# Front stage of a diffusion block: modulation loads in another order, shift 1 added behind the channel DFT

## The reference, cut to what matters

```python
mod = silu(c) @ w_mod + b_mod                      # c: one row of 2048, w_mod: 2048 x 12288 (96 MB)
sh1, sc1, g1, sh2, sc2, g2 = split(mod, 6)         # six vectors of 2048
h = rms_norm(x, norm_g[0]) * (1 + sc1) + sh1
y = real(fft over the 256 tokens and, within each of 8 groups, over 256 channels of h) @ fnet_w
x = x + g1 * rms_norm(y, norm_g[1])
h2 = rms_norm(x, norm_g[2]) * (1 + sc2) + sh2
x = x + g2 * rms_norm(relu(h2 @ w_mlp_in)**2 @ w_mlp_out, norm_g[3])
# second block: projections, two kinds of attention, output projection, MLP, final norm
```

## Time and profile before

| | |
|---|---|
| time, median of 3 runs | 2184.45 us (2181.9 to 2184.6) |
| profiled execution, first to last instruction | 2180.3 us |
| of it ahead of the MLP's steady run (to 308.4 us) | 308.4 us |
| of it after that | 1871.9 us |
| TensorE busy | 2038.3 us, 93% |
| VectorE busy | 1270.9 us, 58% |
| ScalarE busy | 1020.5 us, 47% |
| moved by DMA | 463.03 MB, 212 GB/s on the mean |

### The profile page before, as it was taken

How to read it: one execution, slowest core, us unless ns; L and a number is a source line. 1 busy time by engine, 2 the same in 40 slices (tenths; PEclk the granted TensorE clock), 3 DMA queues, 4 the chain that set the end, 5 groups by cost and what they waited for, 6 DMA issues and landing times.

```text
span 2180.3 us, 24124 instructions
## 1 busy us (share of the span) xinstructions
PE 2038.3 (93%) x9141; PEld 1667.9 (76%) x9141; DVE 1270.9 (58%) x1191; ACT 1020.5 (47%) x1346; POOL 23.0 (1%) x25
## 2 busy tenths in 40 slices
PE   3499469999999999998999999999999999999997
PEld 1378358888888888887778778788888888888886
DVE  7978986555655454456546556654544454454454
ACT  3043245444444544444556654554445444544543
POOL 0000010000000000000000000000000000000000
PEclk9699669999999999999999999999999999999999
DMA  9999977666675555555454454455555555555552
GB/s 400 420 348 358 333 251 252 236 234 242 232 248 174 191 186 194 183 193 174 136 174 159 152 172 143 166 174 193 183 194 187 188 192 192 178 189 194 190 186 103
DMA packets 193757, 463.03 MB, mean 212 GB/s; under 512 B 7401, under 2 KB 7849, under 8 KB 180753
## 3 DMA queue, kind: packets, MB, share of 16 engines
q1 hardware_dynamic: 191808, 455.11, 60.6%
q0 software_dynamic: 848, 3.70, 0.5%
q10 hardware_dynamic: 1024, 3.20, 0.4%
HBM read 459.87 MB, written 2.10 MB: 212 GB/s over the span
## 4 chain that ended last, share of the span: by engine, by line
PE 86%; DVE 9%; ACT 2%; issue 1%; DMA 1%; ACTq 0%; DVEq 0%; SPq 0%
PE ps L419 27%; PE ps L421 27%; PE ps L420 27%; DVE scr L1107 6%; PE ps L455 2%; DVE w_low L1095 1%; DMA raw<-in_w_mod 1%; ACT w_high L779 1%; PE ps L555 0%; PE ps L557 0%; DVE h_both L1186 0%; PE ps L429 0%; PE ps L442 0%; PE ps L449 0%; ACT L993 0%
## 5 line engine op out<-in xcount | busy, mean ns | idle before, releaser
L1095 DVE TENSOR_TENSOR w_low<-raw,w_high 128x1024 fp32r<-128x1024 f32 x672 | 820.8, 1225 | 813.0 <-ACT w_high L779 812.8
L779 ACT ACTIVATE w_high<-raw 128x1024 fp32r<-128x1024 f32 x672 | 708.6, 1059 | 886.5 <-PE ps L421 870.1
L419 PE MATMUL ps<-w_high,h_both 128*128 128x512 f32 x1536 | 610.1, 397 | 8.5 <-DVE w_low L1095 7.6
L421 PE MATMUL ps<-w_high,h_both 128*128 128x512 f32 x1536 | 600.8, 391 | 0.0
L420 PE MATMUL ps<-w_low,h_both 128*128 128x512 f32 x1536 | 600.1, 391 | 0.0
L419 PE MATMUL ps<-w_high,u_high 128*128 128x512 f32 x1152 | 451.0, 392 | 0.3 <-DVE u_low L1489 0.3
L421 PE MATMUL ps<-w_high,u_low 128*128 128x512 f32 x1152 | 448.6, 389 | 0.0
L420 PE MATMUL ps<-w_low,u_high 128*128 128x512 f32 x1152 | 448.3, 389 | 0.0
L419 PEld LDWEIGHTS ps<-w_high,h_both 128*128 128x128 f32 x1536 | 289.8, 189 | 68.6 <-DVE w_low L1095 5.7
L421 PEld LDWEIGHTS ps<-w_high,h_both 128*128 128x128 f32 x1536 | 289.4, 188 | 62.0
L420 PEld LDWEIGHTS ps<-w_low,h_both 128*128 128x128 f32 x1536 | 290.0, 189 | 58.2 <-issue 0.5
(11 more groups left out here) (171 smaller groups left out, 819.9 us busy)
## 6 DMA issues: line engine op xcount, KB each, us to landing
raw<-in_w_mod SPq DMA_DIRECT2D x96, 1024.0 KB, 7.0
raw<-in_w_mlp_in SPq DMA_DIRECT2D x64, 1024.0 KB, 5.7
raw<-in_w_mlp_out SPq DMA_DIRECT2D x64, 1024.0 KB, 5.0
raw<-in_w_up SPq DMA_DIRECT2D x64, 1024.0 KB, 5.5
raw<-in_w_down SPq DMA_DIRECT2D x64, 1024.0 KB, 5.0
raw<-in_w_in SPq DMA_DIRECT2D x48, 1024.0 KB, 5.1
raw<-in_fnet_w SPq DMA_DIRECT2D x16, 1024.0 KB, 6.2
raw<-in_w_out SPq DMA_DIRECT2D x16, 1024.0 KB, 5.0
```

The lines of the kernel that those rows point to most:

```text
L419: eng.matmul(dst, ah, wh, start=(k == 0), stop=False)
L421: last = eng.matmul(dst, al, wh, start=False, stop=(k == KT - 1))
L779: eng.activation(w_high[:, h % LEAD, :], raw[:, slot, (h % 2) * 2 * CW:(h % 2 + 1) * 2 * CW], ACT.Copy).then_inc(high_ready, 1)
L1095: eng.tensor_tensor(w_low[:, h % LEAD, :], raw[:, slot, piece], w_high[:, h % LEAD, :].bitcast(f32), ALU.subtract).then_inc(raw_used if h ...
```

## The change

Five vectors are still accumulated by VectorE ahead of the MLP, from the same 80 tiles, and all 16 fnet chunks are the same. What differs:

- **Order of the vectors**: scale 1, shift 1, gate 1, shift 2, scale 2 (before: shift 1, scale 1, gate 1, shift 2, scale 2). `FRONT` lists all 96 pieces, and SP and VectorE both follow it. The two accumulators simply alternate now.
- **Where the chunks stand**: 34 tiles ahead of the first fnet chunk (before 47), then 1, 1, 2, 1 tiles behind the chunks of each step, 20 in all (before one each behind chunks 2 to 13), then 26 tiles (before 21).
- **Scale 1** is summed by TensorE right behind the token DFT of groups 0 to 6; VectorE takes it (`mod_columns`) behind tile 17. ScalarE's scaling then starts with scale 1 alone, in the instruction that it had before.
- **Shift 1** is summed on TensorE between groups 6 and 7 of the channel DFT. It no longer goes through ScalarE: TensorE transforms it apart with 4 small matmuls (`turn_shift`), and VectorE adds it to `h_high` and `h_low` in 4 small instructions (`add_shift`) ahead of the first fnet chunk. 16 one-column activations (L910) go.
- **Gate 1**'s row sums are made on TensorE behind chunk 9 (`GATE_ROWS = 9`, before 10), after a wait for the last tile of gate 1, which is the second tile behind chunk 10.
- In a column step VectorE now copies the sums before the tile that stands behind the chunk, not after it.
- In the tail, updates and norms stand in groups of two to four behind pairs of tiles.
- GpSimd clears and fills the accumulator of gate 2 once shift 2 has been summed (before: once scale 2 has been).

```diff
-GATE_AHEAD = 15
-FNET_AFTER = range(2, 14)
 SEQ_AHEAD = 5
-GATE_ROWS = 10
-SHIFT_AT = GATE_AHEAD + len(FNET_AFTER) - KT
+GATE_ROWS = 9
+SC1, SH1, G1, SH2, SC2, G2, FNET = range(7)
+MOD_COLUMNS = (1, 0, 2, 3, 4, 5)
+BEHIND_CHUNK = (1, 1, 2, 1)
+FRONT = []
+FRONT += [(unit, kk) for unit in (SC1, SH1) for kk in range(KT)]
+LATER = [(unit, kk) for unit in (G1, SH2, SC2) for kk in range(KT)]
+FRONT += [LATER.pop(0) for _ in range(2)]
+for ch in range(4 * NC):
+    FRONT.append((FNET, ch))
+    FRONT += [LATER.pop(0) for _ in range(BEHIND_CHUNK[ch % 4])]
+FRONT += LATER
+AT = {piece: n for n, piece in enumerate(FRONT)}
...
             for v in range(6):
                 if v >= 2:
-                    eng.wait_ge(mod_read, v if v == 5 else v - 1)
+                    eng.wait_ge(mod_read, v - 1)
...
+            def last_read(unit, kk=KT - 1):
+                t.c["raw"] = AT[unit, kk] + 1
+                eng.wait_ge(raw_used, t.at("raw", 0))
...
+            def turn_shift():
+                eng.wait_ge(mod_cols, 2)
+                for e in range(2):
+                    dst = ps[:, 3, 2 * KT + e * FG:2 * KT + (e + 1) * FG]
+                    for d in range(2):
+                        last = eng.matmul(dst, tables[:, d, e * P:(e + 1) * P],
+                                          shift1[:, :].rearrange("p (g d) -> p d g", d=2)[:, d, :],
+                                          start=(d == 0), stop=(d == 1))
+                last.then_inc(shift_turned, 1)
...
-            for v in range(2):
-                t.add("raw", KT)
-                eng.wait_ge(raw_used, t.c["raw"])
-                sum_partitions_to_columns(v, v)
+            last_read(SC1)
+            sum_partitions_to_columns(SC1, 3)
             for g in range(FG):
                 eng.wait_ge(scaled, g + 1)
...
                 if g >= 2:
                     eng.wait_ge(dft_low, g - 1)
+                if g == FG - 1:
+                    last_read(SH1)
+                    sum_partitions_to_columns(SH1, 1)
...
+            turn_shift()
             eng.wait_ge(dft_low, FG)
-            t.add("raw", GATE_AHEAD)
+            eng.wait_ge(shift_added, 1)
...
                     if hh % 2 and ch == GATE_ROWS:
-                        sum_partitions_to_rows(2)
+                        last_read(G1)
+                        sum_partitions_to_rows(G1)
...
+            for n in range(AT[FNET, 0]):
+                front_tile(n)
+                if n == 4:
+                    t.add("squared", TT * NC)
+                    mean_square()
+                elif n == 5:
+                    invert()
+                elif n == AT[SC1, KT - 1] + 1:
+                    mod_columns(SC1, 3)
+                g = n - (AT[FNET, 0] - FG - 1)
+                if 0 <= g < FG:
+                    eng.wait_ge(dft_high, g + 1)
+                    eng.tensor_tensor(h_low[:, 2 * g:2 * g + 2, :],
+                                      lin(g)[:, 0, :].rearrange("p (e s) -> p e s", e=2),
+                                      h_high[:, 2 * g:2 * g + 2, :].bitcast(f32), ALU.subtract).then_inc(dft_low, 1)
+                if n == AT[SH1, KT - 1] + 1:
+                    mod_columns(SH1, 1)
+            add_shift()
+            for ch in range(4 * NC):
+                t.c["raw"] = AT[FNET, ch]
+                low_part()
+                low_part()
+                if ch == GATE_ROWS + 4:
+                    gate(1)
+                if ch >= 5 and ch % 4 == 1:
+                    t.add("done", 8)
+                    add_step(None, ch // 4 - 1, ch // 4 - 1)
+                if ch == GATE_ROWS + 3:
+                    mod_rows(G1, 1).then_inc(mod_cols, 1)
+                    eng.wait_ge(mod_cols, 3)
+                    gate(0)
+                mod_behind(ch)
```

More of the change, by code:

```diff
@@ L289, in mod_tile @@
             def mod_tile(unit, kk):
-                load(w_mod[bass.ds(kk * P, P), unit * D:(unit + 1) * D])
-            for i in range(RAW):
-                if i == 2:
+                column = MOD_COLUMNS[unit] * D
+                load(w_mod[bass.ds(kk * P, P), column:column + D])
+            for n, (unit, k) in enumerate(FRONT):
+                if n == 2:
                     eng.wait_ge(vec_in, 16 * 8)
[L296 to L314, removed]
+                if unit == FNET:
+                    chunk(fnet_w, k % 4 * 4 * P, k // 4 * CW)
+                else:
+                    mod_tile(unit, k)
             def mlp_chunk(w1, w2, q, ch):
@@ L439, in sum_scale_2_by_quarters @@
                     else:
-                        eng.wait_ge(raw_used, t.c["raw"])
+                        last_read(SC2)
                     for j in range(4 * part, 4 * part + 4):
-                        last = eng.matmul(ps[:, TURN_BANKS[4 + part], j:j + 1],
-                                          mod_acc(4)[:, j * P:(j + 1) * P], ones[:, 0:1], start=True, stop=True)
+                        last = eng.matmul(ps[:, SCALE_BANKS[part], j:j + 1], mod_acc(SC2)[:, j * P:(j + 1) * P],
+                                          ones[:, 0:1], start=True, stop=True)
                     last.then_inc(part_read if part < 3 else mod_read, 1)
@@ L1316, in last_scale_tile @@
                 t.add("raw")
-            behind += [(4, kk) for kk in range(KT)]
-            left = len(behind)
-            for i in range(left):
-                next_tile()
-                if i == 0:
+            for n in range(AT[FNET, 0]):
[15 more added lines that the diff above has]
+                    mod_columns(SH1, 1)
@@ L1324, in _ @@
+            for n in range(AT[SH2, 6], len(FRONT)):
+                front_tile(n)
+                behind = n - AT[SH2, 6]
+                if behind == 1:
                     gate(NC - 2)
-                elif i == 1:
+                elif behind == 4:
+                    t.add("done", 8)
+                    add_step(None, NC - 1, NC - 1)
+                elif behind == 5:
                     gate(NC - 1)
                     mean_square()
-                elif i == 2:
+                elif behind == 7:
@@ L1329, in _ @@
                     invert()
-                elif 3 <= i < 11:
-                    update(i - 3)
-                elif i == 12:
-                    mean_square()
-                elif i == 13:
-                    invert()
-                if 13 <= i < 17:
-                    for piece in range(TT):
-                        normalize(TT * (i - 13) + piece)
-                if i == left - KT + 1:
-                    mod_columns(3, 2)
+                    for i in range(2):
+                        update(i)
+                elif behind == 9:
+                    for i in range(2, 5):
+                        update(i)
+                elif behind == 11:
+                    for i in range(5, 8):
+                        update(i)
+                elif behind == 13:
+                    mean_square()
+                    mod_columns(SH2, SHIFT_BANK)
+                elif behind in (15, 17):
+                    if behind == 15:
+                        invert()
+                    for i in range(4 * (behind // 17), 4 * (behind // 17) + 4):
+                        normalize(i)
```

172 lines of the change are left out of this document (67 added, 105 removed).

## The result

The changed kernel took 2197.57 us (median of 4 runs, 2194.34 to 2200.49), the kernel before, measured beside it, 2183.61 us (median of 4, 2181.9 to 2184.6). The ratio is 1.0059, 95% interval 1.0044 to 1.0075: the change costs 14.0 us. Forecast was 2193.5 us, with 2179 to 2199 as the range, and +9.1 us over before.

A forecast was written before the change was run, and what follows sets the result against it. VectorE's queue was taken to bound the front, loads close behind. Terms -19.2 + 7.6 + 11.8 + 1.0 + 10.9 - 3 gave +9.1 us on 2184.45, so 2193.5 us, range 2179 to 2199.

The forecast's parts named there:

- the forecast's own: Whole kernel: the likeliest case, slower by 3 to 13 us, its own range 2188 to 2198 us; chance 0.57.
- What bounds the front: Stages ahead of fnet: a queue on VectorE, loads close behind; VectorE's standing still before its last tile counts.
- Waits that go, -19.2: VectorE's old waits: 12.8 us for `w_high` and 5.4 for `h_high` go, plus 1 us of register instructions.
- Scale 1, +7.6: Behind tile 17: VectorE stands from 56.7 until the column sum is ready at 64.3 us, 7.6 us.
- Channel DFT, +11.8: Ahead of fnet: TensorE starts group 2 late at fallen clock, so VectorE waits from 110.9 to 122.7, 11.8 us.
- `add_shift`, +1.0: Ahead of the first fnet chunk: four linked VectorE instructions on 16 columns add 1.0 us of work.
- fnet, +10.9: fnet chunks: TensorE waits for row sums, VectorE then for `w_high`, with loads and squares; 10.9 us of waits, end at 227.
- Tail, 0: Last 26 tiles, before 21: moved work already counted, pairing updates and norms gains nothing.
- Turn, -3: Between last tile and MLP: only GpSimd's clearing of `acc` is left to meet a cast, saving 3 us.
- A (fnet keeps up): fnet: TensorE stays two chunks behind VectorE, the 10.9 us of waits go; -1.8 us, 2182.6 us, chance 0.2.
- B (faster): fnet keeps up, and TensorE keeps full clock between DFT groups 1 and 2; -5 us, 2179.5 us, chance 0.13.
- C: fnet: TensorE only 85% busy, dropping to 1.2 GHz repeatedly, two more dips; +16 us, 2200 us, chance 0.1.

The follow-up runs named there:

- the second measurement: The changed kernel run again with no edit, beside the kernel before: median 2195.18 us, ratio 1.0052.
- the kernel with the late clearing: Changed kernel, but GpSimd clears gate 2's accumulator (`scr`) only once scale 2 is summed, as in the kernel before: median 2198.27 us, ratio 1.0064.

## Why the prediction was right, and where its sizes were off

The time, 2197.6 us, is in the range and in the forecast's own (2188 to 2198), 4.1 us above the value given. The difference to before is less near, 14.0 against 9.1 (10.7 in the second measurement): the kernel before ran 0.8 us under the 2184.45 that the forecast started from. The profiled execution, 2200.49 us, lies above the range, and the two largest errors, the channel DFT 3.8 us and the tail 4.3 us too low, both have the sign of this miss. Step by step:

- **What bounds the front.** Right. Taking away each wait on VectorE brought its last tile forward, in every experiment.
- **Waits that go, -19.2.** They were taken off whole and can't be judged apart from the new ones, which are measured below.
- **Scale 1, +7.6.** Measured 9.03. The sum began at 61.40, 0.7 behind the forecast (the token DFT began at 32.80, 0.6 ahead of it, but took 23.89 us and not 22.59), and the 17th tile had ended at 56.04, 0.7 ahead of it. Taking the column later removed the wait, as the trace of that experiment shows.
- **Channel DFT, +11.8.** Measured 15.6. Group 2 began at 87.90 (forecast 87.3). The mis-sized step is "2.7 more for about 5.5 us at half clock": the clock rose, and then fell again during the column sum, which took 5.05 us instead of 3.63, and group 7 ran slowly behind it. Where the sum kept its clock, in the kernel with the late clearing, the wait was 11.8. So the queue was forecast right and a second loss of clock was missed. Of the 3.8 us between the two traces, 3.3 stand ahead of the last low part (7.95 against 4.62), where the sum and group 7 are, and 0.5 ahead of group 2. The unchanged kernel's second trace has 15.2.
- **`add_shift`, +1.0.** Measured 0.75: from 126.14, when the tile ahead of it is done, to 126.89.
- **fnet, +10.9.** Right in size, and in place for the larger half: 104.0 us from the first low part to the end, where 122.7 and 227 make 104.3. TensorE was free at 186.7 (192.88 - 6.19; forecast 182, plus the 4.2 by which it began late) and waited 6.19 us; the row sums took 5.21; VectorE waited 4.26 and 1.44 (forecast 4 and 1.5). Its other waits for `w_high` ahead of there are seven of 0.23 to 1.03 us, 3.8 in all (forecast 3.5, for loads); the 2 us at ScalarE's squares show as 0.24. Moving the rows took the wait away.
- **Tail, 0.** Wrong, the term that was missing: 79.8 us from the end of fnet to the end of the last tile, where 227 and 302.5 make 75.5. Load waits of 4.6 us stand in it (3.08 the largest). I had seen that GpSimd's five transfers leave the turn, and counted only what the turn gains; they are now issued at 270 to 273 us, beside the tiles' loads, which used 0.97 of the DMA already. With the transfers put behind the clearing, VectorE's waits for loads fell back to 3.6 us in all, and to 3.9 where GpSimd clears late; the seven traces with the transfers in the tail have 6.1 to 8.2.
- **Turn, -3.** Measured -3.5; undone, it came back. The forecast had one cast in view, which now takes 3.10 us beside GpSimd's clearing instead of 4.87. The kernel before had a second, beside the clearing of `scr` at 295.55:

```profile
295.59 2.03 DVE L1186 CAST h_both<-extra 128x512 fp32r<-128x512 f32 x1
```

The same cast takes 0.42 us with GpSimd idle, and in the change none meets that clearing: the two casts lose 1.8 and 1.6 us, which is the 3.5 within rounding. The Trainium skill, "SBUF — State Buffer", section "Who interferes with whom", states that of a cast in a two-port mode and a GpSimd instruction the one that issues first has the shared port for its whole length. The trace agrees in that each of the three casts ends 0.3 us behind the end of the clearing beside it.

The end of the last tile was forecast at 302.5 (290.4 + 12.1) and came at 310.7. Of these 8.2 us, 4.2 are there when fnet begins, -0.3 comes in it and 4.3 behind it. The turn gave 0.5 more than forecast and the rest of the program cost 1.6: together the 9.3 us, within the rounding, by which the profiled span's +18.4 exceeds +9.1. The medians differ by less, 14.0 and 10.7 us. One reason is in the choice of the two executions: a run's time stands 1.8 us above its span (2200.49 and 2198.7), not 4.2, so that the profiled one of before was near 2182.1, 1.5 us under its median, and that of after was 2.9 over its own.

Of the rivals, A (fnet keeps up) and B (faster) fell with the 6.19 us wait of TensorE, B also with the weaker clock. C gave nearly the time of the profiled execution, 2200, but not by its mechanism: behind its slow start fnet had one dip, at the row sums, not three (0.95 over the stage).

## What the runs showed of the hardware that I had not expected

**The clock fell while TensorE was busy with one-column matmuls.** The changed kernel, around the column sum of shift 1 (columns as in the earlier trace rows), then the row sums' dip; and the column sum in the kernel with the late clearing:

```profile
111.70:119.00 7.30, 7.06 (x37) 6.73 (x38) 3.05 (x3) 0.57 (x1) 1.80 (x1) 0.66 0.76 263
...
190.00:196.00 6.00, 3.12 (x4) 1.51 (x5) 5.65 (x5) 2.00 (x2) 0.00 (x0) 0.50 0.96 344
```

```profile
110.44 3.70 PE L435 MATMUL ps<-cst,scr 128*128 128x1 f32 x32 [0.31 <-DVE scr L1121]
```

TensorE is busy for 7.06 of 7.30 us and is granted 0.66 of full speed on the mean, a mix of 1.2 and 2.4 GHz. In steps of 2 us it is granted 1.00 to 114.0, in the middle of the sum, and 0.51 from 114 to 116, with TensorE busy all the time. The dip at 190 has the reason that was forecast, a rest ahead of it. The six traces with the sum ahead of group 7 and at most 0.31 us of rest before it run the same instructions there: four took 5.05 to 5.35 us and two 3.70; why these kept the clock is open.

**At the MLP's start the clock may fall back once.** Three microseconds each, the changed kernel and the same kernel in the first series:

```profile
325.00:328.00 3.00, 2.78 (x7) 2.18 (x8) 2.93 (x6) 3.00 (x8) 0.00 (x0) 0.61 0.50 141
328.00:331.00 3.00, 3.00 (x12) 2.45 (x11) 2.93 (x6) 3.00 (x6) 0.00 (x0) 0.82 0.54 208
331.00:334.00 3.00, 3.00 (x15) 2.46 (x15) 3.00 (x4) 2.27 (x3) 0.00 (x0) 1.00 0.41 90
```

```profile
324.00:327.00 3.00, 2.46 (x11) 2.05 (x12) 2.93 (x6) 3.00 (x8) 0.00 (x0) 1.00 0.44 89
327.00:330.00 3.00, 2.75 (x13) 1.95 (x12) 2.93 (x6) 3.00 (x7) 0.00 (x0) 1.00 0.69 261
```

With the full clock TensorE does 11 and 13 matmuls where it otherwise does 7 and 12, and the rest of the program from the last tile on is 1.8 us shorter (1888.9 against 1890.7). It is the same code, so this is a part of the scatter between runs, and no term of the change. The kernel before was granted 0.52 in the first 3 us of its run and 1.00 from there, and its rest, 1871.9 us from the steady run on, lies 1.6 under the changed kernel's and 0.3 over that of the repeat.

**Weight chunks load more slowly than modulation tiles at the same share**, 372 GB/s with 0.98 against 418 to 424. In fnet that is the bound once the waits are out of the way. That it is due to the shorter rows of a chunk was not tried.

## What to carry to other kernels

Where one engine's queue sets the end, add up its waits, and place each pick-up in the queue behind the time at which its result is really there: one column asked for 9 us too early cost some 5 us by the medians, and taking it four tiles later cost nothing. Two reasons for one wait have to be removed together: here each alone gave 1.1 and 2.5 us, no more than the scatter, and both 8.9. And follow everything that a moved wait releases, transfers above all: what leaves one stretch arrives in another, and if the DMA is full there it is paid for.
